# A two-block transformer kernel: the first product takes both token tiles by chunk, and the cross-attention memory is loaded on the weights' queue

## What is computed

```python
# first block, layer 0 (_mixer_ab)
proj = jnp.einsum('bsd,df->bsf', h, w_in)               # 256x1024 by 1024x1440: the first product
c_q, c_kv, k_r, q_s, k_s, v_s = _split_cols(proj, AB_SPLITS)
q = jnp.einsum('bsr,rf->bsf', _rms_norm(c_q, q_norm), w_uq)
kv = jnp.einsum('bsr,rf->bsf', _rms_norm(c_kv, kv_norm), w_ukv)
...
# second block
mem_n = rms_norm(mem, mem_norm_g[layer])                # 256x1024
mk, mv = jnp.split(mem_n @ w_mem_kv, 2, axis=-1)
```

## Time and profile before

| | us |
|---|---|
| median of 3 runs | 919.42 (919.41 to 920.51) |
| the profiled execution | 920.3 |
| its span, first to last instruction | 918.2 |
| TensorE busy | 909.2 |
| VectorE busy | 609.0 |
| ScalarE busy | 508.4 |

### The profile page before, as it was taken

One profiled execution on the slowest core, in us unless ns is written; L12 is line 12 of the kernel. 1 busy time (PEld: TensorE's weight loads), 2 busy tenths in 40 slices (PEclk: granted clock), 3 DMA queues, 4 the chain that ended last, 5 costly groups with the idle time before them and its releaser, 6 DMA issues.

```text
span 918.2 us, 12819 instructions
## 1 busy us (share of the span) xinstructions
PE 909.2 (99%) x4766; PEld 765.4 (83%) x4766; DVE 609.0 (66%) x1003; ACT 508.4 (55%) x819; POOL 36.1 (4%) x53
## 2 busy tenths in 40 slices
PE   8999999999999999999999999999999999999997
PEld 7888888888888898878888888887888888888886
DVE  4788687666663767778766666376656577574665
ACT  4885564655553455666465555255457564655444
POOL 1100034000000001000000000001000000000000
PEclk9999999999999999999999999999999999999999
DMA  8754456755564668454755557454564555555651
GB/s 295 256 204 138 138 196 207 257 191 192 190 232 135 140 190 258 125 164 153 272 170 193 190 190 235 135 192 143 186 204 138 161 191 164 174 157 183 197 172 70
DMA packets 72557, 169.39 MB, mean 184 GB/s; under 512 B 11305, under 2 KB 33217, under 8 KB 71857
## 3 DMA queue, kind: packets, MB, share of 16 engines
q1 hardware_dynamic: 69536, 155.83, 51.9%
q0 software_dynamic: 2816, 12.48, 4.0%
q10 hardware_dynamic: 144, 0.26, 0.1%
HBM read 167.49 MB, written 1.06 MB: 184 GB/s over the span
## 4 chain that ended last, share of the span: by engine, by line
PE 95%; DVE 2%; DMA 1%; ACT 1%; issue 1%; SPq 0%; DVEq 0%; ACTq 0%
PE psum L740 21%; PE psum L927 15%; PE psum L688 8%; PE psum L693 8%; PE psum L690 8%; PE psum L931 7%; PE psum L960 6%; PE psum L965 3%; PE psum L851 3%; PE psum L861 3%; PE psum L855 3%; PE psum L1062 2%; PE psum L660 1%; PE psum L1093 1%; PE psum L1076 1%; PE psum L1018 1%
## 5 line engine op out<-in xcount | busy, mean ns | idle before, releaser
L1640 DVE TENSOR_TENSOR base_lo<-stage,base_hi 128x1024 fp32r<-128x1024 f32 (+3 forms) x222 | 262.0, 1204 | 94.5 <-ACT base_hi L1246 93.4
L1246 ACT CAST base_hi<-stage 128x1024 fp32r<-128x1024 f32 (+3 forms) x222 | 224.0, 1035 | 54.5 <-PE psum L693 25.1
L1640 DVE TENSOR_TENSOR extra_lo<-stage,extra_hi 128x1024 fp32r<-128x1024 f32 (+1 forms) x68 | 80.0, 1202 | 48.1 <-ACT extra_hi L1246 47.6
L688 PE MATMUL psum<-base_hi,xt 128*128 128x512 f32 (+2 forms) x272 | 107.2, 394 | 0.8 <-ACT base_hi L1246 0.5
L690 PE MATMUL psum<-base_lo,xt 128*128 128x512 f32 (+2 forms) x272 | 104.7, 385 | 1.0 <-DVE base_lo L1640 0.7
L693 PE MATMUL psum<-base_hi,xt 128*128 128x512 f32 (+2 forms) x272 | 104.7, 385 | 0.0
L1246 ACT CAST extra_hi<-stage 128x1024 fp32r<-128x1024 f32 (+1 forms) x68 | 68.2, 1031 | 49.3 <-PE psum L740 30.8
L740 PE MATMUL psum<-base_hi,ht 128*128 128x512 f32 x288 | 87.4, 394 | 0.0
L927 PE MATMUL psum<-xt,extra_hi 128*128 128x512 f32 x320 | 87.3, 394 | 0.0
L960 PE MATMUL psum<-xt,base_hi 128*128 128x512 f32 x240 | 76.5, 403 | 0.0
L927 PE MATMUL psum<-xt,base_hi 128*128 128x512 f32 x256 | 69.8, 394 | 0.0
(11 more groups left out here) (243 smaller groups left out, 1550.2 us busy)
## 6 DMA issues: line engine op xcount, KB each, us to landing
stage<-in_w_up SPq DMA_DIRECT2D x80, 512.0 KB, 4.4
stage<-in_w_down SPq DMA_DIRECT2D x44, 512.0 KB, 4.6
stage<-in_w_in_a SPq DMA_DIRECT2D x22, 512.0 KB, 4.6
stage<-in_w_cd_in SPq DMA_DIRECT2D x16, 512.0 KB, 4.6
stage<-in_w_in_b SPq DMA_DIRECT2D x12, 512.0 KB, 3.7
stage<-in_w_ab_in SPq DMA_DIRECT2D x11, 480.0 KB, 7.4
ln_par<-in_ln POOLq DMA_DIRECT2D x4, 1024.0 KB, 6.9
stage<-in_w_ab_out SPq DMA_DIRECT2D x8, 512.0 KB, 3.6
```

The source lines that it names most:

```text
L688: pe.matmul(acc, ah, wh, start=(k == 0), stop=False)
L1246: act.copy(w_hi(c, 0, w), stage_of(c, w)).then_inc(hi_done, 1)
L1640: dve.tensor_tensor(w_lo(c, 0, w), stage_of(c, w), w_hi(c, 0, w).bitcast(F32), ALU.subtract).then_inc(lo_done, 1)
```

## The change

x is loaded in three parts on SP's queue: the left half (512 columns) of tile 0, the identity, the left half of tile 1, and behind chunk 1 both right halves in one load. TensorE turns the left halves of both tiles, then does four matmuls on ones instead of two, and then `token_step`, which replaces the tile-by-tile step: k = 0, k = 1, then k in pairs; for each group first high weights by high tokens of both tiles, then high weights by low tokens, then low weights by high tokens. The right halves are turned inside the group of k = 2 and 3, behind its first four products. ScalarE and VectorE copy the turned halves in the same order: left halves, chunk 0, chunk 1, right halves, chunks 2 and 3. The loads of `mem`, `mem_g` and `gains` move from GpSimd's queue to SP's, behind the load of chunk 7. GpSimd loads `swa` and `rope` when ten high parts are made. Memory's norm moves from place 5 (behind chunk 8's split) to place 4 (ahead of chunk 7's) on both engines. Nothing is added to or taken from the arithmetic; the sums run in another order.

```diff
 SP
-            load_x(0)
+            load_left(0)
             sp.dma_start(ident[:, :], d["ident"]).then_inc(loaded["ident"], 16)
+            load_left(1)
...
-                    if g.c0 + n == NS - 1:
-                        load_x(1)
+                    if g.c0 + n == 1:
+                        load_right()
+                    if g.c0 + n == 2 * NS - 1:
+                        load_memory()
+            def load_left(t):
+                sp.dma_start(x[:, t, 0:512], d["x"][t * P:(t + 1) * P, 0:512]).then_inc(loaded[f"x{t}"], 16)
+
+            def load_right():
+                sp.dma_start(x[:, :, 512:1024], d["x"].rearrange("(t p) n -> p t n", t=TT)[:, :, 512:1024]
+                             ).then_inc(loaded["x_right"], 16)
+
+            def load_memory():
+                for name, dst, src in (
+                        ("mem", mem_x, d["mem"].rearrange("(t p) n -> p t n", t=TT)),
+                        ("mem_g", row_g[:, :], row(d["mem_norm_g"], D)),
+                        ("gains", gains, row(d["gains"], Q_RANK + KV_RANK))):
+                    sp.dma_start(dst, src).then_inc(loaded[name], 16)
 GpSimd
             pool.wait_ge(hi_done, NS)
-            load("mem_g", row_g[:, :], row(d["mem_norm_g"], D))
-            load("mem", mem_x, d["mem"].rearrange("(t p) n -> p t n", t=TT))
-            load("gains", gains, row(d["gains"], Q_RANK + KV_RANK))
             load("heads", head_par[:, :, :].rearrange("p a h -> p (a h)"), row(d["head_par"], 16))
-            pool.wait_ge(hi_done, 2 * NS)
+            pool.wait_ge(hi_done, 2 * NS + 2)
             load("swa", table, d["swa"])
 TensorE
+        token_parts = [(2 * q + t, t, 4 * q, 4) for q in range(2) for t in range(TT)]
-            def turn_tokens(t):
-                turn("x0", tile_of(x), [(loaded[f"x{t}"], 16)], [t])
-                if t == 0:
-                    ones_by_ones(2)
+            for part, landed in zip(token_parts, ("x0", "x1")):
+                turn_part(part, "x0", tile_of(x), [(loaded[landed], 16)])
+            ones_by_ones(4)
+
+            def turn_right():
+                for part in token_parts[TT:]:
+                    turn_part(part, "x0", tile_of(x), [(loaded["x_right"], 16)])
+            def token_step(name, turn_right):
+                g = PRODUCTS[name]
+                def high(k, src, made):
+                    c, kk = g.c0 + k // g.kp, k % g.kp
+                    pe.wait_ge(*((hi_done, c + 1) if k else (first_hi, 1)))
+                    for t in range(TT):
+                        pe.wait_ge(made, 1 + 2 * (k // 4) + t)
+                        pe.matmul(psum[:, 2 * (g.u0 % 2) + t, 0:g.n], src[:, k, t * P:(t + 1) * P],
+                                  w_hi(c, kk * g.n, g.n), start=(k == 0 and made is turn_hi), stop=False)
+                def low(k):
+                    c, kk = g.c0 + k // g.kp, k % g.kp
+                    pe.wait_ge(*((lo_done, c + 1) if k else (first_lo, 1)))
+                    for t in range(TT):
+                        last = pe.matmul(psum[:, 2 * (g.u0 % 2) + t, 0:g.n], xt_hi[:, k, t * P:(t + 1) * P],
+                                         w_lo(c, kk * g.n, g.n), start=False, stop=(k == g.kc - 1))
+                    if kk == g.kp - 1:
+                        last.then_inc(chunk_used, 1)
+                for ks in ((0,), (1,), (2, 3), (4, 5), (6, 7)):
+                    for k in ks:
+                        high(k, xt_hi, turn_hi)
+                    if ks[0] == 2:
+                        turn_right()
+                    for k in ks:
+                        high(k, xt_lo, turn_lo)
+                    for k in ks:
+                        low(k)
-            gemm("ab_in", xt_hi, xt_lo, 0, "x0",
+            token_step("ab_in", turn_right)
+            gemm("ab_in", xt_hi, xt_lo, 0, None,
...
-                 second=turn_tokens)
+                 first=1)
 ScalarE
-            first, last = turn_parts("x0", [0])
-            turn_part(first, "x0")
+            for part in token_parts[:TT]:
+                turn_part(part, "x0")
             act.wait_ge(first_staged, 16)
             act.copy(w_hi(0, 0, FIRST), stage_of(0, FIRST)).then_inc(first_hi, 1)
-            turn_part(last, "x0")
             act.wait_ge(staged[STAGE[0]], 16)
             act.copy(w_hi(0, FIRST, FIRST), stage_of(0, WIDTH[0])[:, FIRST:]).then_inc(hi_done, 1)
             done["chunks"] = 1
+            split_to(2)
+            for part in token_parts[TT:]:
+                turn_part(part, "x0")
             split_to(NS)
-            turn("x0", xt_hi, 0, [1])
-                 {5: lambda: [split_to(done["due"]), memory_norm()], 7: ...
+                 {4: memory_norm, 7: ...
 VectorE: the same edits as ScalarE, with the subtractions
```

More of the change, by code:

```diff
@@ L318, in build_program, with row @@
         QK_BANK, LOGIT_BANK, PT_BANK, O_BANK = 4, 5, 6, 7
+        token_parts = [(2 * q + t, t, 4 * q, 4) for q in range(2) for t in range(TT)]
+        def row(src, n):
+            return bass.AP(tensor=src.tensor, offset=src.offset, ap=[[0, P], [1, n]])
         def turn_bank(name, g):
@@ L366, in build_program @@
         final_rest = sem("final_rest")
-        loads = ["x0", "x1", "ident", "mem_g", "mem", "gains", "rope", "swa", "masks", "heads", "ln0", "ln1", "ln2",
+        loads = ["x0", "x1", "x_right", "ident", "mem_g", "mem", "gains", "rope", "swa", "masks", "heads", "ln0", "ln1", "ln2",
                  "ln3",
@@ L661, in turn_part, with step @@
                 last.then_inc(turned, 1)
-            def step(g, j, hi, lo, k0=0, turned_by=None, between=None, second=None):
+            def step(g, j, hi, lo, k0=0, turned_by=None, between=None):
                 u, cps = g.u0 + j, g.kc // g.kp
                 pair = u % 2
[L668 to L697, removed]
@@ L699, in gemm @@
-            def gemm(name, hi, lo, k0=0, turned_by=None, between=None, second=None, first=0):
+                if u >= 2:
+                    pe.wait_ge(acc_free[pair], 2 * (u // 2))
+                for m in range(cps):
+                    n = j * cps + m
+                    c = g.c0 + n
+                    for kk in range(g.kp):
+                        k = m * g.kp + kk
+                        wh, wl = w_hi(c, kk * g.n, g.n), w_lo(c, kk * g.n, g.n)
+                        for t in range(TT):
+                            turn_of = turned_by is not None and j == 0 and turned_at(turned_by, t, k)
+                            acc = psum[:, 2 * pair + t, 0:g.n]
+                            ah, al = hi[:, k0 + k, t * P:(t + 1) * P], lo[:, k0 + k, t * P:(t + 1) * P]
+                            pe.wait_ge(hi_done, c + 1)
+                            if turn_of:
+                                pe.wait_ge(turn_hi, turn_of)
+                            pe.matmul(acc, ah, wh, start=(k == 0), stop=False)
+                            pe.wait_ge(lo_done, c + 1)
+                            pe.matmul(acc, ah, wl, start=False, stop=False)
+                            if turn_of:
+                                pe.wait_ge(turn_lo, turn_of)
+                            last = pe.matmul(acc, al, wh, start=False, stop=(k == g.kc - 1))
+                    last.then_inc(chunk_used, 1)
+                    if between and n in between:
+                        between[n]()
@@ L700, in gemm @@
+            def gemm(name, hi, lo, k0=0, turned_by=None, between=None, first=0):
                 g = PRODUCTS[name]
                 for j in range(first, g.steps):
-                    step(g, j, hi, lo, k0, turned_by, between, second=second if j == 0 else None)
+                    step(g, j, hi, lo, k0, turned_by, between)
+            def token_step(name, turn_right):
[10 more added lines that the diff above has]
+                    pe.wait_ge(*((lo_done, c + 1) if k else (first_lo, 1)))
+                    for t in range(TT):
+                        last = pe.matmul(psum[:, 2 * (g.u0 % 2) + t, 0:g.n], xt_hi[:, k, t * P:(t + 1) * P],
+                                         w_lo(c, kk * g.n, g.n), start=False, stop=(k == g.kc - 1))
+                    if kk == g.kp - 1:
+                        last.then_inc(chunk_used, 1)
+                for ks in ((0,), (1,), (2, 3), (4, 5), (6, 7)):
[7 more added lines that the diff above has]
+                        low(k)
@@ L1477, in _ @@
             gemm("ab_in", copy_to(lambda j, t, acc: (proj0[:, t, j * 480:(j + 1) * 480], acc[:, 0:480])),
-                 {5: lambda: [split_to(done["due"]), memory_norm()], 7: lambda: [turn("mem", ht_hi, 0, [0]), low_rank_norms()],
+                 {4: memory_norm, 7: lambda: [turn("mem", ht_hi, 0, [0]), low_rank_norms()],
                   8: lambda: turn("mem", ht_hi, 0, [1]),
@@ L1972, in split_first @@
                                          w_hi(0, m * FIRST, FIRST).bitcast(F32), ALU.subtract)
-            turn_part(first, xt_hi, xt_lo, 0, "x0")
+            for part in token_parts[:TT]:
+                turn_part(part, xt_hi, xt_lo, 0, "x0")
```

(7 more changed lines are left out.)

4 lines of the change are left out of this document (removed).

## The result

| | before | after |
|---|---|---|
| median, 10 runs each | 919.75 us | 922.92 us |
| ratio, 95% interval | | 1.0030 (1.0019 to 1.0042) |
| span of the profiled execution | 918.2 us | 921.1 us |

The change made the kernel slower, by 3.2 us. The forecast was 2.1 us faster.

The account below looks back on a forecast made before the run. TensorE, busy 909.2 of 918.2 us, was taken as the bound, with holes at the start. A 2.8 us gain less a 0.7 us hole gave 2.1 us, so 917.3 us; own range 916.8 to 918.0, 8 in 10 916.2 to 918.9.

Parts of the forecast that it names:

- Part 1 and 2: Token loads and first product by chunk: chunk 1 0.4 us later, both tiles by chunk, second step 2.8 us sooner.
- E: Moment the first product ends and step 2's first matmul begins: 22.36 before, forecast 19.6, bounds 19.2 to 20.2.
- The wait for it at 10.83: TensorE's wait before k = 2 for chunk 1's high part, forecast done at 10.83 instead of 10.43.
- two more ones: Two extra matmuls on ones before k = 0: about 0.9 us, costing nothing because a wait for chunk 1 covers them.
- The gain of 2.8: Start of the kernel: step 2 begins 2.8 us sooner, 19.6 instead of 22.36, taken off the span and the median.
- Part 3: Memory's loads on SP's queue behind chunk 7: mem issued at 17.15, moved at 403 GB/s, landing at 22.8.
- Part 4: Norm ahead of chunk 7's split: 5.5 us from mem's landing, low part at 28.3, wanted at 27.6, hole 0.7 us.
- The clock: TensorE's granted clock, 1.00 from 7.25 to 11.63: a hole costs its own length and no clock.
- Rival three: Memory's wait blocks chunk 7: at 251 GB/s mem lands at 25.8, hole 3.7 us, 0.9 slower, 920.3; chance 0.06.
- Its other price, 923.0: Same blocking case with mem's old 11.4 us: landing 28.5, hole 6.4, net 3.6 us slower; within the chance 0.06.
- Keep their distances: Memory's transposes and all behind them are released by engines, so they shift together, 2.1 us sooner.

Follow-up runs that it names:

- e5_memory_only: Kernel before with only the memory part: mem, mem_g, gains on SP's queue behind chunk 7, norm at place 4; 919.46 us against 919.66, ratio 0.9998.
- e8_early_place5: Changed kernel with mem, mem_g, gains issued behind chunks 4, 5, 6, heads behind the tenth high part, norm at place 5; 917.56 us against 919.66, ratio 0.9969.
- e2_heads_late: Changed kernel with GpSimd's 8 KB load of heads moved behind the tenth high part; 921.44 us against 919.58 before, ratio 1.0013.
- e9_early_heads: e8_early_place5 with GpSimd's small load of heads back where the changed kernel has it; 917.58 us against 919.66 before, ratio 0.9972.
- e1_norm5: Changed kernel with memory's norm back at place 5, behind chunk 8's split; 922.12 us against 919.58 before, ratio 1.0020.
- a0_after: The changed kernel itself run again, as yardstick on the same chip; 923.35 us against 919.94 before, ratio 1.0030.
- e4_head_only: Changed kernel keeping only the new first product and token loads; memory's loads on GpSimd's queue and norm at place 5 as before; 918.75 us against 919.58, ratio 0.9987.
- e7_early_place4: Changed kernel with mem, mem_g, gains issued behind chunks 4, 5, 6, heads behind the tenth high part, norm at place 4; 918.61 us against 919.66, ratio 0.9981.

## Why the prediction was wrong

- **Part 1 and 2, the first product: the moment right, in part by luck.** E was said at 19.6 and came at 19.64. But chunk 1 was not 0.4 later: it was cast from 8.64 instead of 9.39, for it landed at 3.13 + 5.5 = 8.6. The wait for it at 10.83, 0.1 us as said, did not come (k = 2 began at 10.75). The start at 8.06, said as 8.1, is luck: the 0.9 us for two more ones was too much (it counts from the weight load at 6.32, the first of these matmuls stands at 6.53 in the earlier trace rows; now eight records took 1.06 us), and a wait of 1.0 us for the left half of the second tile (4.5 us from issue to landing) was not foreseen. From 10.75 on the steps came within 0.2 us of those said.
- **The gain of 2.8 is probably too large against the median.** The forecast took all of it off the median, though it had been read from an execution 0.9 us longer. In e5_memory_only, whose start is that of the kernel before, step 2 began at 21.36 and the span is 1.0 us shorter. So the extra time of the profile seems to have lain in this very start, and about 2 us is what a median run can gain. e8_early_place5, 2.1 faster by the medians and 2.9 by the spans, fits that; two profiles don't prove it.
- **Part 3, mem's landing: the step that failed.** Said 22.8, measured 16.89 + 9.0 = 25.9, outside the 22.3 to 24 that the prediction allowed; those 3.1 us are 3.1 us more of hole. The issue was right (17.15). I took the rate of a stretch in which SP's chunk loads alone kept the engines full (403 GB/s, share 1.00) and set aside the 251 GB/s that the same stretch of the program showed, because GpSimd's queue was mixed in there; but the changed kernel still had GpSimd's small load at just that point. The rate while the three transfers moved, in the changed kernel and then in e2_heads_late:

```profile
17.00:23.40 6.40, 6.40 (x31) 5.54 (x31) 2.79 (x3) 1.91 (x3) 0.00 (x0) 1.00 0.90 255
```

```profile
17.00:23.40 6.40, 6.40 (x31) 5.56 (x30) 2.92 (x3) 1.95 (x4) 0.00 (x0) 1.00 0.90 306
```

255 GB/s is nearly the 251 that was set aside. With the small load moved it is 306, still not 403: from 16.0 to 23.4 the engines moved 2.05 MB, as much as the three transfers hold (2.03), and mem landed 1.3 later, at 24.7. So the small load is 0.5 to 1.2 us of the 3.1 (by the two profiles of the changed kernel), and the rest is the rate of these loads themselves, put too high. Why they move at 306 here stays open. From issue to landing this 1 MB load on SP's queue took 7.0 to 9.0 us in all twelve profiles that have it there (7.0 in e9_early_heads, 9.0 in the changed kernel), not 5.7.
- **Part 4: right.** From mem's landing to chunk 7's low part 5.5 us were said; 25.9 + 5.5 = 31.4, and TensorE got it at 31.5. The hole before the low part was named, with its place and its releaser; that with a later mem the high part would be late too (2.1 us of the wait) was not. In the sum: 0.7 us of hole were said, 2.29 + 1.59 = 3.9 came.
- **The clock: missing.** I wrote that a hole costs its own length and no clock, from a window whose holes were under 1.3 us. Behind 4.1 us of near idleness it cost 1.7 more. Rival three had the right mechanism and nearly the right landing (25.8), and gave 0.9 us slower; with 1.7 for the clock it would have been 2.6, where 3.2 was measured (2.9 in the span). (Its other price, 923.0, is close to the measured 922.92, but by a landing at 28.5 and no clock; that is chance.) Its chance of 0.06 was far too low: a case that the rate seen in the same stretch of the program leads to isn't a rare one.
- **"Keep their distances": right.** From 35.58 on the changed kernel's profile keeps 2.85 to 2.9 us of delay to the end.

## To carry over

When a change moves a consumer sooner, ask of each load that is released by something else whether it comes sooner too, or even later, and what is queued behind the instruction that waits for it; here two parts that were harmless alone lost 3.2 us together. Price a load by its time from issue to landing in the crowd it will be in, not by the best bandwidth of the trace, and if the two lie 3 us apart, give the bad case the weight of a forecast. A wait of TensorE can cost more than its length, so put a possibly late transfer behind work that can go on, as e8_early_place5 does.

## What the runs showed of the hardware

- With one 8 KB load of GpSimd's queue, spread over 128 partitions from one short row and issued at 15.2 to 15.8, the window from 18.0 to 20.4 moved 61 to 112 GB/s in five profiles; with it later, 276 and 238. It isn't always so: issued at 17.45 behind three others of its queue it made no standstill (307), and issued at 15.49 beside an SP queue filled earlier it left 262 (e9_early_heads).
- Behind a hole of 2.9 us (e1_norm5), or of two with one matmul between (2.1 and 1.3 us in the changed kernel, 1.5 and 1.3 in a0_after, 0.9 and 1.3 in e2_heads_late), the granted clock was 0.50 to 0.58 over the next 3.4 to 4.6 us; behind a single hole of 1.1 or 1.3 us (e4_head_only, e7_early_place4) it stayed at 1.00. What it costs varies: eleven matmuls took 4.05 to 4.57 us instead of 2.4.
- Whether rows of 2 KB delay the weights behind them the profiles don't tell: chunk 1 was cast from 8.64 to 9.58 in twelve profiles with rows of 2 KB, and at 9.39 and 8.40 in the two with rows of 4 KB (the kernel before, e5_memory_only).
